# Gated DeltaNet stage: block sums and decay masks moved on VectorE, signs moved to ScalarE

## The chip, the cores and the metric

The kernel runs on one core of a Trainium2 chip. The metric is the device time of one execution in microseconds (us); the figure given is the median of several. All matrix products are in 32-bit floats.

## The reference

A backbone of two layers over 256 latent and 256 context tokens, D_MODEL 1024. Each layer is SwiGLU, token mixer, SwiGLU, with norms and modulation. The mixer of the first layer is a bidirectional gated DeltaNet with 8 heads of width 128. The change is in its scan, whose core for one head and one direction is, in the reference:

```python
Gamma = jnp.exp(jnp.where(incl, G[..., :, None] - G[..., None, :], -jnp.inf))
A = jnp.where(strict, jnp.einsum('nbhcd,nbhsd->nbhcs', kb, kc) * Gamma, 0.0)
Tinv = lax.linalg.triangular_solve(eye + A, jnp.broadcast_to(eye, A.shape), left_side=True,
                                   lower=True, unit_diagonal=True)
u = jnp.einsum('nbhcs,nbhse->nbhce', Tinv, vc * bc[..., None])
intra = jnp.einsum('nbhcd,nbhsd->nbhcs', qc, kc) * Gamma
```

and then a scan over chunks that carries a 128x128 state. The output is the latent stream.

## The kernel before

The kernel takes the 512 tokens in four chunks of 128 (the reference has chunks of 64; the result is the same) and both directions d = 0, 1 together. For each head it needs, in this order: the decays and their masked copies; the gram products of keys and queries (`gram_pair`, L1221); the unit-triangular inverse; the state scan over four chunks; the output.

**The inverse** is built in two steps. On VectorE, all 8x8 diagonal blocks are solved at once: GpSimd masks the blocks (`below`, L626), VectorE sums them into packed rows (`pack_rows`, L2661, one sum for each direction, and a subtraction, L2667), GpSimd spreads these (L640, L642), TensorE broadcasts them (`spread_blocks`, L1230), and VectorE runs `solve`: a copy (L2671) and seven pairs of small instructions (L2675, L2676), each behind the last. `place_base` writes the result as base blocks and transposes it (L2683, L2687). Then four levels double the block width: 8, 16, 32, 64. At each level q, TensorE forms a product (`level_p1`), VectorE masks or copies it (`mask_p1`), TensorE forms a second product (`level_y`), and the result, with its sign changed, enters the inverse (`update_y`). For widths 8 and 16 that is a subtraction and a transpose on packed blocks (L2714, L2715). At width 32 (q = 2) the packed blocks are unpacked into the full matrices `yy` and `tt_`: ScalarE places the diagonal blocks (`place_t`, `place_y`, L1818) and copies the transposed off-diagonal block with scale -1 (`copy_t`, L1837); VectorE writes the off-diagonal blocks with scale -1 (`negated`, L2707, 32 rows by 128, two for each direction). At width 64 (q = 3) VectorE writes the off-diagonal half (L2722, 64 rows by 256, one for each direction). "Signs" below are these instructions with scale -1.

**The rounds.** Every engine runs its own program of ten rounds (`rounds(delta_round)`). In round i four heads are in work: n = i prepares (decays, grams, block solve), g = i - 1 goes through the four levels, h = i - 2 goes through the state scan, f = i - 3 closes. Each round is a loop over q = 0 to 3, and in it the order of the work of the four heads on each engine is written out by hand. Heads are 0 to 7, so rounds 3 to 7 have all four, round 1 has n and g only, round 8 has no n, rounds 9 and 10 no n and no g. In round 1 (g = 0), TensorE also computes the last gate projections between the levels (`late_gate`, L1210), and ScalarE their exponentials (`gate_exp`).

What sets the order around the change are semaphores. `level_p1(g, q)` waits for the base blocks (q = 0), for VectorE's update of the level before, or, at q = 3, for `t_copied` and `y_updated`. `turn_v` and `turn_k` (TensorE transposes, L1305, L1296) wait for `intra_done`, since they write over the banks of the gram products that `make_intra` (L2602) reads. ScalarE's `scale_v` (L1848) and `copy_k` (L1843) follow, and TensorE's `spread_decays` of the next round (L1165) waits for them. ScalarE's `exp_sums` (L1700) and `bound` (L1706) follow that, and `gram_pair` waits for `bounded`. `new_values(h, 0)` (L1324), the start of a head's scan, waits for all the updates of its inverse. On GpSimd the order is: decays times beta (L621), the masked blocks (L626), the masked decays (L631), the two spreads (L640, L642), the decayed queries (L647). The solve's output goes to the same tile in which the level below width 32 works, so `place_base` waits for `place_y` of the head before.

Of the kernel before, what the change touches and what calls it, by code (L numbers as in the profile page):

```python
# [9 lines left out]
ALU = mybir.AluOpType  # L10
# [4 lines left out]
P = 128  # L15
# [198 lines left out]
def hybrid_backbone(nc, x, c, ctx_in, c_ctx, w_mod, b_mod, norm_pre, norm_post, ffn_w_in, ffn_w_out,  # L214
# [13 lines left out]
    with ExitStack() as ctx:  # L228
# [437 lines left out]
        def _(pe):  # L666
# [143 lines left out]
            for n, (kind, l, j) in enumerate(SUBS):  # L810
# [261 lines left out]
                if kind == "gdn":  # L1072
# [159 lines left out]
                    def level_p1(g, q):  # L1232
                        for d in range(2):
                            if q == 0:
                                of("base_done", g, 1, 1)
                            elif LEVELS[q] <= QUARTER:
                                of("y_updated", g, 2 * n_lev, 2 * (q - 1) + d + 1)
                            else:
                                of("t_copied", g, 2, d + 1)
                                of("y_updated", g, 2 * n_lev, 2 * (q - 1) + d + 1)  # L1240
# [328 lines left out]
        def _(act):  # L1569
# [70 lines left out]
            for n, (kind, l, j) in enumerate(SUBS):  # L1640
# [51 lines left out]
                if kind == "gdn":  # L1692
# [139 lines left out]

                    def copy_t(g):
                        for d in range(2):
                            r, o = quarters(d, d)
                            of("t_done", g, 2, d + 1)
                            fn(chunks(tt_[quarter_rows[o], d, :])[:, :, quarter_rows[r]],  # L1837
                               bank[quarter_rows[o], d, 3 * P:4 * P].rearrange("p (t c) -> p t c", t=NC), ACT.Copy, scale=-1.0
                               ).then_inc(S["t_copied"], 1)
# [36 lines left out]
                    def delta_round(n, g, h, f):  # L1876
# [3 lines left out]
                        for q in range(n_lev):  # L1880
# [11 lines left out]
                            if g is not None and q == 3:  # L1892
                                scale_v(g)
                                copy_k(g)
# [191 lines left out]
        def _(dve):  # L2086
# [223 lines left out]
            for n, (kind, l, j) in enumerate(SUBS):  # L2310
# [180 lines left out]
                if kind == "gdn":  # L2491
# [212 lines left out]
                    def negated(g, d, k):  # L2704

                        r, o = quarters(d, k)
                        return v_.tensor_scalar(chunks(yy[g % 2][quarter_rows[r], d, :])[:, :, quarter_rows[o]],  # L2707
                                                by_chunk(bank[quarter_rows[r], d, 2 * P:3 * P]), -1.0, None, ALU.mult)

                    def update_y(g, q):  # L2710
                        for d in range(2):
                            of("y_done", g, 2 * n_lev, 2 * q + d + 1)
                            if LEVELS[q] < QUARTER:
                                steps.link(v_.tensor_tensor(yq[d], yq[d], bank[:, d, 0:P], ALU.subtract))  # L2714
                                last = v_.transpose(tq[d], yq[d])  # L2715
                            elif LEVELS[q] == QUARTER:
                                last = negated(g, d, 1 - d)
                                last.then_inc(S["y_updated"], 1)
                                negated(g, d, d)
                                continue  # L2720
                            else:
                                last = v_.tensor_scalar(chunks(yy[g % 2][rows_of[d], d, :])[:, :, rows_of[1 - d]],  # L2722
                                                        by_chunk(bank[rows_of[d], d, 0:NC * HALF]), -1.0, None, ALU.mult)
                            last.then_inc(S["y_updated"], 1)
# [32 lines left out]
                    def delta_round(n, g, h, f):  # L2757
                        for q in range(n_lev):
# [4 lines left out]
                            if n is not None and q == 3:  # L2763
                                solve(n)
                            if n is not None and q == 1:
# [3 lines left out]
                            if g is not None:  # L2769
# [3 lines left out]
                            if n is not None and q == 2:  # L2773
                                pack_rows(n, 1)
                            if f is not None and q == 2:
                                close(f)
                            if n is not None and q == 2:
                                make_intra(n)
                            if g == 0 and q < 3:
                                gate_scale(4 + q)  # L2780
                        if n is not None:
                            place_base(n)
# [228 lines left out]
```

## Time and profile before

| | us |
|---|---|
| median of 3 runs | 2312.84 (2311.76 to 2315.14) |
| the profiled execution | 2312.73 |
| its span | 2311.0 |
| granted TensorE clock, mean of the span | 0.983 |
| TensorE matmul busy | 2217.4 (96%) |
| VectorE busy | 1343.4 (58%) |
| ScalarE busy | 609.2 (26%) |
| GpSimd busy | 169.7 (7%) |

The ten rounds of the delta stage run from about 695 to 917 us of the span. In the profile PE is TensorE's matmul, PEld its weight load, DVE VectorE, ACT ScalarE, POOL GpSimd; times of a row are microseconds from the span's start and durations in us, unless marked ns. A granted clock of 1.00 is 2.4 GHz, 0.50 is 1.2 GHz. In `128*128 128x256 f32` the first pair is the part of the array that is used. `[1.15 <-X]` says that the engine stood idle for 1.15 before this row, and that X released it.

### The profile page before, as it was taken

Reading aid. Unit: us, or ns where it says so; the run is one execution under the profiler, and the core shown is the slowest. Engines: PE = TensorE matmul, PEld = TensorE weight load, DVE = VectorE, ACT = ScalarE, POOL = GpSimd, SP = SyncE. Lnnn points to the kernel's source line nnn. Section 1 sums busy time; section 2 is a strip of 40 time slices with the busy share of each in tenths; the row PEclk is TensorE's granted clock in tenths of the full one; section 3 lists DMA queues with packets and bytes.
Section 4 is the critical chain, followed back from the end, with each engine's and each line's share of the span. In section 5 each row is a group of like instructions: output and inputs, shape, how many; then the busy total and the mean of one; then the engine's idle time right before and its main releaser. Section 6 shows DMA issues by size and latency. Waiting matters only on the chain.

```text
span 2311.0 us, 39267 instructions
## 1 busy us (share of the span) xinstructions
PE 2217.4 (96%) x15693; PEld 1916.7 (83%) x15693; DVE 1343.4 (58%) x2258; ACT 609.2 (26%) x1635; POOL 169.7 (7%) x236
## 2 busy tenths in 40 slices
PE   5999999999998888999999999999999999879998
PEld 3788889988865776888888998888899868569997
DVE  4377758666774885267775865767556421735521
ACT  2111111132344766321111123111111311632210
POOL 1100000000022441000000000000000000000000
PEclk7999999999999999999999999999999999989999
DMA  8555557532220000225554763455456332024462
GB/s 299 184 173 169 174 146 205 151 118 79 73 79 26 3 3 15 84 92 167 170 175 127 206 180 114 147 164 167 135 137 176 103 105 91 1 73 148 163 186 69
DMA packets 311486, 293.38 MB, mean 127 GB/s; under 512 B 6713, under 2 KB 292019, under 8 KB 311219
## 3 DMA queue, kind: packets, MB, share of 16 engines
q1 hardware_dynamic: 290611, 215.90, 31.4%
q0 software_dynamic: 20736, 75.51, 10.5%
q8 instruction: 102, 1.67, 0.3%
q14 instruction: 37, 0.30, 0.0%
HBM read 290.34 MB, written 1.05 MB: 126 GB/s over the span
## 4 chain that ended last, share of the span: by engine, by line
PE 89%; DVE 4%; ACT 3%; DMA 2%; issue 1%; SPq 0%; POOL 0%; DVEq 0%; POOLq 0%; ACTq 0%
PE bank L864 39%; PE bank L986 18%; PE bank L718 6%; PE bank L1092 5%; PE bank L1064 3%; PE bank L1445 2%; PE bank L828 2%; PE bank L1210 1%; PE bank L1147 1%; DMA mring<-in_w_mod 1%; PE bank L1221 1%; PE bank L696 1%; PE bank L1082 1%; ACT hs L1932 1%; PE bank L754 1%
## 5 line engine op out<-in xcount | busy, mean ns | idle before, releaser
L864 PE MATMUL bank<-hs,ring 128*128 128x256 f32 (+1 forms) x2112 | 446.1, 356 | 6.3 <-ACT hs L1617 5.1
L864 PEld LDWEIGHTS bank<-hs,ring 128*128 128x128 f32 x2112 | 365.5, 192 | 55.3 <-issue 11.3
L986 PE MATMUL bank<-big,ring 128*128 128x128 f32 x2904 | 330.2, 275 | 0.0
L986 PEld LDWEIGHTS bank<-big,ring 128*128 128x128 f32 x2904 | 327.4, 192 | 0.2
L864 PE MATMUL bank<-room,big 128*128 128x256 f32 (+1 forms) x1408 | 296.0, 353 | 0.0
L864 PEld LDWEIGHTS bank<-room,big 128*128 128x128 f32 x1408 | 242.4, 191 | 26.5
L2134 DVE SCALAR_TENSOR_TENSOR mring<-mring,cond 128x1024 f32<-128x1024 f32 x196 | 240.2, 1278 | 7.6 <-DMA mring<-in_w_mod 7.6
L603 POOL DMA_DIRECT2D mring<-in_w_mod x144 | 76.6, 532 | 1062.9 <-DVE mring L2128 488.3
L864 PE MATMUL bank<-room,ring 128*128 128x256 f32 (+1 forms) x704 | 149.3, 355 | 2.5 <-ACT room L1653 1.8
L864 PEld LDWEIGHTS bank<-room,ring 128*128 128x128 f32 x704 | 121.0, 190 | 20.0 <-ACT room L1653 6.8
L1657 ACT ACTIVATE room<-room 128x256 f32<-128x256 f32 (+1 forms) x88 | 34.3, 390 | 302.6 <-DVE room L2339 302.6
L2870 DVE TENSOR_TENSOR room<-room 128x256 f32<-128x256 f32 x70 | 29.5, 421 | 132.5 <-ACT room L1977 131.9
L2329 DVE TENSOR_TENSOR room<-room,bank 128x256 f32<-128x256 f32 (+1 forms) x88 | 34.0, 387 | 119.2 <-ACT room L1653 118.0
L986 PE MATMUL bank<-room,ring 128*128 128x128 f32 x792 | 95.1, 276 | 1.1 <-ACT cst L2042 1.1
L1653 ACT ACTIVATE room<-bank 128x256 f32<-128x256 f32 (+1 forms) x88 | 31.5, 358 | 237.5 <-PE bank L864 237.5
L986 PEld LDWEIGHTS bank<-room,ring 128*128 128x128 f32 x792 | 91.3, 192 | 1.7 <-ACT cst L2042 1.7
L718 PE MATMUL bank<-big,ring 128*128 128x256 f32 x384 | 89.4, 396 | 2.6 <-POOL big L662 1.8
L718 PEld LDWEIGHTS bank<-big,ring 128*128 128x128 f32 x384 | 76.1, 200 | 14.5 <-POOL big L662 2.2
L2334 DVE TENSOR_TENSOR big<-cst,bank 128x256 f32 (+3 forms) x88 | 33.9, 386 | 86.1 <-PE bank L864 86.0
L864 PE MATMUL bank<-hs,big 128*128 128x256 f32 (+1 forms) x384 | 80.8, 353 | 0.2 <-DVE room L2329 0.2
L2526 DVE SCALAR_TENSOR_TENSOR room<-room,prm 128x512 f32<-128x512 f32 x96 | 76.1, 792 | 3.1
L1064 PE MATMUL bank<-big,ring 128*128 128x256 f32 x352 | 77.3, 379 | 0.0
(355 smaller groups left out, 3252.2 us busy)
## 6 DMA issues: line engine op xcount, KB each, us to landing
ring<-in_ffn_w_in SPq DMA_DIRECT2D x88, 1024.0 KB, 5.7
ring<-in_ffn_w_out SPq DMA_DIRECT2D x56, 1408.0 KB, 7.2
mring<-in_w_mod POOLq DMA_DIRECT2D x144, 512.0 KB, 4.0
ring<-in_gdn_w_in SPq DMA_DIRECT2D x16, 1024.0 KB, 5.6
ring<-in_diff_w_in SPq DMA_DIRECT2D x12, 1024.0 KB, 5.2
ring<-in_gdn_w_out SPq DMA_DIRECT2D x4, 1024.0 KB, 5.5
ring<-in_diff_w_out SPq DMA_DIRECT2D x4, 1024.0 KB, 5.2
cst<-in_consts SPq DMA_DIRECT2D x1, 1344.0 KB, 10.2
```

Of the source, the lines that this page charges most:

```text
L603: pool.dma_start(mring[:, k % slots, :], w_mod[l, k * P:(k + 1) * P, ds(v * D + (i0 - 9 * l) * D, D)]).then_inc(m_landed[k % slots], 16)
L718: last = mm(bank[0:rows, r % 4, 0:cols], w[:, k, :], rhs(k), start=(k == 0), stop=(k == n_k - 1))
L828: last = mm(bank[:, g % 4, cols], w[:, k, :], hs[:, k, cols], start=(k == 0), stop=(k == KC - 1), skip_group_check=True)
L864: last = mm(bank[:, (g0 + b) % 4, 0:width], w[:, k, jj * P:(jj + 1) * P], rhs[:, k, 0:width], start=start and k == 0, stop=(k == KC // 2 - ...
L986: last = mm(bank[:, (go + b) % 4, 0:P], w[:, k, :], rhs[:, k, :], start=start and k == 0, stop=(k == FH - 1), skip_group_check=True)
L1064: last = mm(bank[:, g % 4, 0:LAT], w[:, k, :], big[:, k, cols], start=(k == 0), stop=(k == FC - 1))
L1092: last = mm(bank[:, (g0 + b) % 4, 0:LAT], w[:, k, :], rhs[:, k, :], start=start and k == 0, stop=(k == KC // 2 - 1), skip_group_check=True)
L1445: last = mm(bank[:, g % 4, 0:256], hs[:, k, t * P:(t + 1) * P], slot(ux, KC, 256)[:, k, :], start=(k == 0), stop=(k == KC - 1))
L1657: fn(u2c[c % 2][:, 0:width], u2c[c % 2][:, 0:width], ACT.Silu).then_inc(S["gate2_done"], 1)
L2134: last = v_.scalar_tensor_tensor(m_acc[:, v, :], w, scalar, m_acc[:, v, :], ALU.mult, ALU.add)
L2329: v_.tensor_tensor(u4c[c % 2][:, 0:width], u4c[c % 2][:, 0:width], bank[:, (g0 + 3) % 4, 0:width], ALU.add).then_inc(S["c22_added"], 1)
L2526: last = v_.scalar_tensor_tensor(o, conv_in[:, u % 4, :, t:t + LAT], tap(t), o, ALU.mult, ALU.add)
```

## The change

On VectorE, both block sums now stand right behind the copies of level 2; the state update comes ahead of the width-32 signs; the decay masks (`make_intra`) move from the end of q = 2 to q = 3, ahead of the solve; the base blocks move from the end of the round to right behind the solve. Of the width-32 signs VectorE keeps one for each direction, the other goes into ScalarE's `copy_t`, ahead of the signal `t_copied`. The last level's signs go to a new function `place_last` on ScalarE, ahead of `scale_v`. On TensorE the waits follow: level 3's first product waits for `t_copied` alone, and the first level waits also for the last signs of the head before. What is computed stays the same.

```diff
--- before.py
+++ after.py
@@ -1233,11 +1233,12 @@
                         for d in range(2):
                             if q == 0:
                                 of("base_done", g, 1, 1)
+                                if g:
+                                    of("y_updated", g - 1, 2 * n_lev, 2 * (n_lev - 1) + d + 1)
                             elif LEVELS[q] <= QUARTER:
                                 of("y_updated", g, 2 * n_lev, 2 * (q - 1) + d + 1)
                             else:
                                 of("t_copied", g, 2, d + 1)
-                                of("y_updated", g, 2 * n_lev, 2 * (q - 1) + d + 1)
                             for t in range(NC):
                                 if LEVELS[q] < QUARTER:
                                     for r in range(4):
@@ -1830,12 +1831,23 @@
                                 last = in_place(yy[g % 2], yq[d], d, r)
                             last.then_inc(S["y_placed"], 1)
 
+                    def place_last(g):
+                        for d in range(2):
+                            of("y_done", g, 2 * n_lev, 2 * (n_lev - 1) + d + 1)
+                            fn(chunks(yy[g % 2][rows_of[d], d, :])[:, :, rows_of[1 - d]],
+                               bank[rows_of[d], d, 0:NC * HALF].rearrange("p (t c) -> p t c", t=NC), ACT.Copy, scale=-1.0
+                               ).then_inc(S["y_updated"], 1)
+
                     def copy_t(g):
                         for d in range(2):
                             r, o = quarters(d, d)
                             of("t_done", g, 2, d + 1)
                             fn(chunks(tt_[quarter_rows[o], d, :])[:, :, quarter_rows[r]],
-                               bank[quarter_rows[o], d, 3 * P:4 * P].rearrange("p (t c) -> p t c", t=NC), ACT.Copy, scale=-1.0
+                               bank[quarter_rows[o], d, 3 * P:4 * P].rearrange("p (t c) -> p t c", t=NC), ACT.Copy, scale=-1.0)
+                            r, o = quarters(d, 1 - d)
+                            of("y_done", g, 2 * n_lev, 2 * (n_lev - 2) + d + 1)
+                            fn(chunks(yy[g % 2][quarter_rows[r], d, :])[:, :, quarter_rows[o]],
+                               bank[quarter_rows[r], d, 2 * P:3 * P].rearrange("p (t c) -> p t c", t=NC), ACT.Copy, scale=-1.0
                                ).then_inc(S["t_copied"], 1)
 
                     def copy_k(g):
@@ -1890,6 +1902,7 @@
                                 copy_t(g)
                                 place_y(g)
                             if g is not None and q == 3:
+                                place_last(g)
                                 scale_v(g)
                                 copy_k(g)
                             if n is not None and q == 0:
@@ -2701,12 +2714,6 @@
                                 last = v_.tensor_copy(p1m[rows_of[1 - d], d, 0:NC * HALF], bank[rows_of[1 - d], d, 0:NC * HALF])
                             last.then_inc(S["p1_masked"], 1)
 
-                    def negated(g, d, k):
-
-                        r, o = quarters(d, k)
-                        return v_.tensor_scalar(chunks(yy[g % 2][quarter_rows[r], d, :])[:, :, quarter_rows[o]],
-                                                by_chunk(bank[quarter_rows[r], d, 2 * P:3 * P]), -1.0, None, ALU.mult)
-
                     def update_y(g, q):
                         for d in range(2):
                             of("y_done", g, 2 * n_lev, 2 * q + d + 1)
@@ -2714,13 +2721,9 @@
                                 steps.link(v_.tensor_tensor(yq[d], yq[d], bank[:, d, 0:P], ALU.subtract))
                                 last = v_.transpose(tq[d], yq[d])
                             elif LEVELS[q] == QUARTER:
-                                last = negated(g, d, 1 - d)
-                                last.then_inc(S["y_updated"], 1)
-                                negated(g, d, d)
-                                continue
-                            else:
-                                last = v_.tensor_scalar(chunks(yy[g % 2][rows_of[d], d, :])[:, :, rows_of[1 - d]],
-                                                        by_chunk(bank[rows_of[d], d, 0:NC * HALF]), -1.0, None, ALU.mult)
+                                r, o = quarters(d, d)
+                                last = v_.tensor_scalar(chunks(yy[g % 2][quarter_rows[r], d, :])[:, :, quarter_rows[o]],
+                                                        by_chunk(bank[quarter_rows[r], d, 2 * P:3 * P]), -1.0, None, ALU.mult)
                             last.then_inc(S["y_updated"], 1)
 
                     def rest(h, st):
@@ -2761,25 +2764,24 @@
                             if g is not None:
                                 mask_p1(g, q)
                             if n is not None and q == 3:
+                                make_intra(n)
                                 solve(n)
+                                place_base(n)
                             if n is not None and q == 1:
                                 make_m2(n)
                             if n is not None and q == 2:
                                 pack_rows(n, 0)
-                            if g is not None:
+                                pack_rows(n, 1)
+                            if g is not None and q < 2:
                                 update_y(g, q)
                             if h is not None and q < NC - 1:
                                 next_state(h, q)
-                            if n is not None and q == 2:
-                                pack_rows(n, 1)
+                            if g is not None and q == 2:
+                                update_y(g, q)
                             if f is not None and q == 2:
                                 close(f)
-                            if n is not None and q == 2:
-                                make_intra(n)
                             if g == 0 and q < 3:
                                 gate_scale(4 + q)
-                        if n is not None:
-                            place_base(n)
                         if n == 1:
 
                             dve.wait_ge(S["acc_done"], gz + KC)
```

## Rows read from the trace of the kernel before

**Rows 1.** Page, the chain that ended last, shares of the span by engine.
```profile
PE 89%; DVE 4%; ACT 3%; DMA 2%; issue 1%; SPq 0%; POOL 0%; DVEq 0%; POOLq 0%; ACTq 0%
```

**Rows 2.** Windows: length; busy (count) of PE, PEld, DVE, ACT, POOL; clock; DMA share, GB/s.
```profile
722.40:731.00 8.60, 8.60 (x27) 4.22 (x28) 0.95 (x3) 2.68 (x9) 0.00 (x0) 0.61 0.00 0
812.20:836.40 24.20, 21.25 (x470) 18.14 (x473) 19.78 (x59) 17.11 (x64) 10.69 (x10) 1.00 0.01 3
```

**Rows 3.** Chain that ended last, in order of time: start, us, what.
```profile
764.26 0.46 DVE room L2687
...
883.29 0.46 DVE room L2687
```

**Rows 4.** Timeline of VectorE, round 5: start, us, line, operation, count, idle before.
```profile
824.00 1.22 DVE L2707 TENSOR_SCALAR room<-bank 32x128 f32<-32x128 f32 x4
...
826.08 1.06 DVE L2661 TENSOR_REDUCE room<-ring 128x32 f32<-128x512 f32 x1
...
827.92 1.28 DVE L2602 TENSOR_TENSOR hs<-bank,hs 128x512 f32<-128x512 f32 x2
...
830.55 0.65 DVE L2671 COPY room<-cst 128x64 f32<-128x64 f32 x1
...
834.49 0.88 DVE L2722 TENSOR_SCALAR room<-bank 64x256 f32<-64x256 f32 x2
835.40 0.43 DVE L2683 TENSOR_TENSOR room<-room,cst 128x256 f32<-128x256 f32 x1
```

**Rows 5.** Timeline of GpSimd, round 5.
```profile
827.49 0.63 POOL L640 TENSOR_TENSOR ring<-room,cst 128x256 f32<-128x256 f32 x1 [3.51 <-DVE room L2667]
...
828.66 2.50 POOL L647 TENSOR_TENSOR hs<-big,hs 128x512 f32<-128x512 f32 x2
```

**Rows 6.** Timeline of VectorE, rounds 1 and 2: the copy that opens the solve.
```profile
724.37 0.18 DVE L2671 COPY room<-cst 128x64 f32<-128x64 f32 x1
...
758.36 1.24 DVE L2671 COPY room<-cst 128x64 f32<-128x64 f32 x1
```

**Rows 7.** Timeline of TensorE, round 5 and the start of round 6.
```profile
826.64 0.96 PE L1254 MATMUL bank<-room,mring 64*64 64x64 f32 x16
828.75 1.12 PE L1230 MATMUL bank<-ring,cst 128*128 128x512 f32 x2 [1.15 <-POOL ring L642]
...
833.18 1.14 PE L1165 MATMUL bank<-cst,pack 128*128 128x128 f32 x8
...
836.36 0.75 PE L1244 MATMUL bank<-room,mring 32*32 32x32 f32 x64 [0.16 <-DVE room L2687]
...
837.92 1.99 PE L1221 MATMUL bank<-big 128*128 128x256 f32 x8
```

**Rows 8.** Lines L1837 and L1843: count, ns min/median/max, first and last start, form.
```profile
L1837 ACT ACTIVATE room<-bank x16: 268/268/269, 722.1 to 895.3; 32x128 f32<-32x128 f32 x16
...
L1843 ACT ACTIVATE room<-bank x4: 614/614/615, 738.5 to 880.4; 128x512 f32<-128x512 f32 x4
```

**Rows 9.** Timeline of ScalarE, round 5.
```profile
825.33 0.56 ACT L1837 ACTIVATE room<-bank 32x128 f32<-32x128 f32 x2
...
831.98 1.14 ACT L1848 ACTIVATE big<-bank,pack 128x128 f32<-128x128 f32 x4 [1.22 <-PE bank L1305]
...
834.85 2.17 ACT L1706 ACTIVATE mring<-bank,pack 128x128 f32<-128x128 f32 x8
```

**Rows 10.** Timeline of TensorE, round 1.
```profile
722.39 1.60 PE L1254 MATMUL bank<-room,mring 64*64 64x64 f32 x16 [3.54 <-ACT room L1837]
723.92 6.23 PE L1210 MATMUL bank<-hs,ring 128*128 128x512 f32 x8
...
731.82 3.70 PE L1210 MATMUL bank<-hs,ring 128*128 128x512 f32 x8
...
738.66 1.52 PE L1165 MATMUL bank<-cst,pack 128*128 128x128 f32 x8 [2.26 <-ACT big L1848]
```

**Rows 11.** Timeline of ScalarE, round 8.
```profile
895.62 2.55 ACT L1818 ACTIVATE hs<-room 32x128 f32<-32x128 f32 x8
```

## The prediction

> **What bounds it now.** I read the page first. TensorE holds 89% of the chain that ended last, VectorE 4% [rows 1]; that is an average over stages, and says nothing of the stage that the diff touches. The windows by stage come next: in one round of the delta stage (812.2 to 836.4) all of TensorE, VectorE and ScalarE work 17 to 21 of 24.2 us, and the granted clock is 1.00 [rows 2]. No engine is full, so the chain decides. In it a round ends each time with VectorE's solve, the last level's two signs (L2722), the base blocks (L2683) and their transpose (L2687), and the next round's first level (L1244) starts behind them. From the transpose of round 2 to that of round 7, 764.26 to 883.29, are five rounds: 23.8 us each [rows 3]. So in rounds 2 to 7 what VectorE does from level 2 on, without a pause, sets the length; in the first third of a round it waits for TensorE, and nothing of that third changes. Rounds 1 (gate projections on TensorE between the levels) and 8 (no solve) are of another kind.
>
> **The steady round (rounds 3 to 7), in round 5's times.** I lay VectorE's work in the new order from the copies of level 2 on (end at 822.9).
> 1. Both block sums now stand there, 1.06 and a step each [rows 4], with their subtraction, until 825.3: about the time that the first block sum and four signs took before (825.2). The state update behind them came at 825.23 and comes at 825.3; its second half waits for TensorE until 825.82 as before. Their input, GpSimd's masked blocks, was ready before the first sum ran, so nothing new is waited for.
> 2. The four width-32 signs take 1.22 [rows 4], 0.305 each. Two remain, two go to ScalarE: **0.61** saved.
> 3. The last level's two signs go to ScalarE: from their start at 834.49 to that of the base blocks at 835.40, **0.91** saved [rows 4].
> 4. The solve's first instruction, a copy of 64 columns, takes 0.65 in round 5 (start 830.55, next 831.23), 1.24 in round 2, but 0.18 in round 1 [rows 4, 6]. In round 5 it ends just where GpSimd's product for the decayed queries ends (828.66 + 2.50 = 831.16), in round 1 GpSimd had long done its own [rows 4, 5, 6]. That product stands behind two short spreads (from 827.49 on) that wait for the block sums [rows 5]. The second sum ended at 827.14 and now ends at 825.06, so the spreads and the product move up by 2.08, to an end near 829.1. The copy will start at about 829.95 and find GpSimd idle: 0.68 falls to 0.20, **0.48** saved. Bounds: 0 and 0.48.
> 5. The decay masks (1.20 for two, L2602) move from ahead of the third state step to ahead of the solve. VectorE pays the same there, so 0. Who waits for them? TensorE's transposes of v and k. By this count the masks end at 829.95, and TensorE gets there at 830.2: the block broadcast (L1230), which stood 1.15 waiting for GpSimd until 828.75 [rows 7], starts at once at 827.6, and new values and level 3 follow without a gap. Their cover is thin, 0.2.
> 6. The base blocks stand right behind the solve; they need the level-3 placement on ScalarE done (near 829.0) and start near 833.4. Cost 0. The first level's new wait for the last signs on ScalarE (done near 830.7) is long over by then.
>
> Steps 2 to 4 sum to 2.00: the next round's first level starts at 834.37, not 836.36 [rows 7].
>
> **What ScalarE takes on.** Width-32 signs: 32x128 from PSUM has rows, 0.268, and a pair takes 0.56 [rows 8, 9]. The 64x256 sign has none; between 0.268 (128 columns) and 0.614 (512 columns) [rows 8] the line by columns gives 0.383, which I take, as duration follows columns; the ends stay for the range. Queued behind the width-32 signs: the placements of the diagonal (eight, 2.55), now ending at 829.03, ahead of level 3's second half at 829.6. Ahead of level 3's first product, the copies end at 826.45, and TensorE arrives at 826.64 [rows 7]: hidden by 0.19. Queued behind the last signs: the scaling of v, the copy of k, and the next round's exponentials. The signs end near 830.65, v is turned at 830.87, so they are hidden by 0.2. The scaling ends at 832.0 where it ended at 833.1 [rows 9], so the spreading of decays (833.18) comes at 832.07: 1.1 earlier, while the round's start comes 2.0 earlier. **ScalarE thus lags 0.9 more behind the start of the round.** Its bound step (L1706, 834.85 for 2.17) ended 0.66 behind the start and will end 1.55 behind it; the gram products that wait for it started 1.56 behind it (837.92 less 836.36) [rows 7, 9]. That is zero cover; I book 0.1. The decays that it makes after that feed GpSimd and through it VectorE's products, whose slack is larger than this lag: 0. A steady round gains **1.9**, five of them **9.5**.
>
> **Round 2.** 0.61 + 0.91, and from the copy 1.07 (1.27 less 0.20) = 2.59. Level 3's product on TensorE is then waited for briefly, about 0.2 by its rows there: **2.4** saved. GpSimd's product would end at about 757.85 and the copy start at about 757.8: no more than 0.1.
>
> **Round 1 loses.** The chain goes through ScalarE twice. Level 3 waited for the copies until 722.39 [rows 10]; each direction's signal now comes behind one more sign: **+0.28**. At its end ScalarE's last gate exponential, the scaling of v, and the spreading at 738.66 follow one another [rows 10]; the two last-level signs stand between, 2 x 0.383: **+0.77**. VectorE's 0.91 is no gain there, since its base blocks were early, and the moved masks fall into 6 us of its idle time.
>
> **Round 8 loses a little.** There is no solve, so the last signs are on the path either way. The placements on ScalarE ended at 898.17 [rows 11], and level 3's second half started near then; two signs ahead of them move it by 0.5, and v's scaling with it: **+0.5**. No DMA and no queue of SP is touched; GpSimd only starts earlier; what follows the stage moves as a whole.
>
> **Sum.** -9.5 - 2.4 + 0.28 + 0.77 + 0.5 = -10.35. The profiled execution took 2312.73 (its span 2311.0 and 1.73 around it): 2302.4. It lies 0.1 below the median of the runs, so 2302.4 stands against 2312.84.
>
> The Trainium skill says (GPSIMD Engine Reference, Specifications) that GpSimd shares its SBUF interfaces with VectorE, and contends with VectorE instructions that have two SBUF inputs as well as with those in a two-port mode. By that rule too the copy is freed. It could speak against the change, since GpSimd's product now runs beside other VectorE work; but each VectorE instruction of that stretch has an operand in PSUM, so the rule adds nothing to the sum, and the trace agrees so far as the copy alone of the instructions beside that product differs from one round to the next; no row here has an instruction with two SBUF inputs beside it.
>
> **Rivals.**
> *A. The copy stays slow* (its wait comes from something else, or GpSimd moves up less). For it: only the ends agree, no row shows the cause. Against: the 0.18 of round 1. Time: 5 x 0.48 + 1.07 = 3.5 less gain, 2305.9.
> *B. ScalarE becomes the bound at the round's head.* For it: the cover ahead of the gram products is zero. If a 64x256 sign costs 0.614, the pair is 0.46 longer; 0.2 is covered, 0.26 is paid in six rounds and 0.46 in round 1: 2304.4. With as much again of lag from late transposes: 2306.5.
> *C. Nothing left to gain*: another wait of the first third grows by what the end of the round saves (say a chain over ScalarE from one round's v to the next round's gram products is 1.5 longer than I count). For it: three engines all work 17 to 21 us of a round. Against: each wait counted above. Time: 2311 to 2314.
> *D. Slower: TensorE's clock.* In round 1 the pause of 3.54 ahead of level 3 was followed by 8.6 us at a mean clock of 0.61, between 1.2 and 2.4 GHz and so for most of them at 1.2 [rows 2, 10]. There the gate products took 6.23 for eight, against 3.70 a little later, and level 3 took 1.60, against 0.96 in round 5 [rows 7, 10]: a fall costs 3.2. The change lengthens this pause by 0.28 and the one of 2.26 at 736.4 by 0.77. If the new pattern of pauses made the clock fall once a round, six falls would cost 19 and the time would be 2321. It decides from four falls on (10.35 / 3.2). Against it: in steady rounds the longest pause was 1.2 at a clock of 1.00 [rows 2, 7], and it gets shorter.
> The Trainium skill has a rule that speaks for D (TensorE: Matmul & The Clock Gate, HAM oscillation): a matmul stream with recurring waits can swing between the two clock levels. The trace agrees in round 1 and not in rounds 3 to 7; by the rule alone D would be as likely as not, and the rows make it unlikely.
>
> **Chances.** Forecast 0.72, A 0.09, B 0.10, C 0.05, D 0.04. A run-to-run difference of about 0.2% (4.6 us) is what a measurement of this kernel can tell. Faster by more: forecast, A, B: 0.91. Within 0.2%: 0.05. Slower: 0.04. The range starts below the forecast by one fall of the clock that may fail to come in round 1 (3.2) and the 0.1 per round, 2299, and goes up to B's second figure and a little over A, 2307.
>
> **What would show it.** Rounds 3 to 7 at 21.9 each between the transposes L2687; the solve's copy at 0.18 in rounds 3 to 7; the 64x256 signs on ScalarE near 0.38; no wait of TensorE for GpSimd ahead of the block broadcast; gram products 1.6 behind the start of the round; VectorE busy some 14 us less in the whole (two signs of 0.29 and two of 0.42 in eight rounds, and the copies' 3.5). I am wrong if the gram products start over 2 behind it, if the transposes of v wait for the masks for over 0.3, or if the clock is below 1.00 in a steady round.

## The result and the profile after

The changed kernel takes 2299.04 us (median of four executions, 2296.22 to 2301.93) against 2312.3 (median of four of the kernel before). The ratio of the two is put at 0.9938, with a 95% interval of 0.9923 to 0.9953: 14.3 us faster, 10.9 to 17.8 (the medians are 13.3 apart). The forecast was 10.35 us faster and a time of 2302.4, in a range that began at 2299.0. The sign was right and the gain was larger than forecast; the profiled execution itself took 2301.93, within half a microsecond of the forecast. The 3 us and more between the forecast and the medians are what the experiments had to find.

The page after (span and instructions; busy time of the engines; the chain that ended last by engine):

```profile
span 2300.2 us, 39265 instructions
...
PE 2217.7 (96%) x15693; PEld 1917.3 (83%) x15693; DVE 1328.2 (58%) x2226; ACT 618.6 (27%) x1667; POOL 169.7 (7%) x236
...
PE 90%; ACT 3%; DVE 3%; DMA 2%; issue 1%; SPq 0%; POOL 0%; DVEq 0%; POOLq 0%; ACTq 0%
```

VectorE is busy 15.2 less (forecast 14), ScalarE 9.4 more. Line numbers have moved: L2725 is the width-32 sign that VectorE kept, L1849 the one that ScalarE took, L1837 the last level's signs, L2684 the copy that opens the solve, L2700 the transpose of the base blocks, L1245 the first level.

VectorE's timeline in round 5 (from the transpose at 806.83 to that at 828.55), beside [rows 4]:

```profile
817.57 2.07 DVE L2674 TENSOR_REDUCE room<-ring 128x32 f32<-128x512 f32 x2
...
820.50 0.35 DVE L2743 SCALAR_TENSOR_TENSOR hs<-hs,pack,bank 128x128 f32<-128x128 f32 x1 [0.32 <-PE bank L1341]
820.76 0.60 DVE L2725 TENSOR_SCALAR room<-bank 32x128 f32<-32x128 f32 x2
...
823.43 1.27 DVE L2615 TENSOR_TENSOR hs<-bank,hs 128x512 f32<-128x512 f32 x2
824.63 0.18 DVE L2684 COPY room<-cst 128x64 f32<-128x64 f32 x1
...
828.10 0.43 DVE L2696 TENSOR_TENSOR room<-room,cst 128x256 f32<-128x256 f32 x1
828.55 0.45 DVE L2700 STREAM_TRANSPOSE room<-room 128x256 f32<-128x256 f32 x1
```

Each term of the forecast's steady round is there: two signs in place of four, the copy at 0.18, no last-level signs. The round takes 21.72, where an undisturbed round of before took 23.72: 2.00 less, which is the sum of steps 2 to 4. Rounds 3 and 4 of this profile are longer, 22.19 and 21.97. ScalarE and TensorE in the same round:

```profile
820.45 0.27 ACT L1849 ACTIVATE room<-bank 32x128 f32<-32x128 f32 x1
...
824.42 0.78 ACT L1837 ACTIVATE room<-bank 64x256 f32<-64x256 f32 x2
825.45 1.14 ACT L1860 ACTIVATE big<-bank,pack 128x128 f32<-128x128 f32 x4 [0.25 <-PE bank L1306]
```

```profile
822.23 1.11 PE L1230 MATMUL bank<-ring,cst 128*128 128x512 f32 x2
...
829.05 0.75 PE L1245 MATMUL bank<-room,mring 32*32 32x32 f32 x64 [0.82 <-DVE room L2700]
...
830.61 1.56 PE L1221 MATMUL bank<-big 128*128 128x256 f32 x6
```

The pair of 64x256 signs (L1837) takes 0.78 (twice 0.383 was 0.77), the scaling of v still waits for TensorE behind it, the block broadcast waits for nobody, and the gram products start 1.56 behind the round's start, as in [rows 7].

Round 1, TensorE's timeline, beside [rows 10]:

```profile
722.15 1.60 PE L1255 MATMUL bank<-room,mring 64*64 64x64 f32 x16 [3.81 <-ACT room L1849]
723.68 6.26 PE L1210 MATMUL bank<-hs,ring 128*128 128x512 f32 x8
...
739.27 1.97 PE L1165 MATMUL bank<-cst,pack 128*128 128x128 f32 x8 [3.07 <-ACT big L1860]
```

The two pauses grew from 3.54 to 3.81 and from 2.26 to 3.07: +0.27 and +0.81, where +0.28 and +0.77 were forecast.

### The profile page after: what moved, and what is told of

The parts are those of the page before. It is cut to its first block, busy times and chain, and to the rows that moved or that the text cites. A ratio compares the mean times of both kernels' runs of the same rounds, so it can differ in the third digit from the quotient of the medians.

```text
span 2300.2 us, 39265 instructions
## 1 busy us (share of the span) xinstructions
PE 2217.7 (96%) x15693; PEld 1917.3 (83%) x15693; DVE 1328.2 (58%) x2226; ACT 618.6 (27%) x1667; POOL 169.7 (7%) x236
## 4 chain that ended last, share of the span: by engine, by line
PE 90%; ACT 3%; DVE 3%; DMA 2%; issue 1%; SPq 0%; POOL 0%; DVEq 0%; POOLq 0%; ACTq 0%
PE bank L864 40%; PE bank L986 18%; PE bank L718 6%; PE bank L1092 5%; PE bank L1064 3%; PE bank L1446 2%; PE bank L828 2%; PE bank L1210 1%; PE bank L1147 1%; DMA mring<-in_w_mod 1%; PE bank L1221 1%; PE bank L696 1%; PE bank L1082 1%; ACT hs L1945 1%; PE bank L754 1%
```

## The experiments

### More profiles of both kernels, to see what differs from one execution to the next

The changed kernel once more, with five executions:

> The changed kernel once more. Its profiled execution took 2301.9, near the 2302.4 forecast, while the median of its four executions is 2299.0 and their granted clocks went from 0.982 to 0.986. Theory (the clock): the missing 3 us are no work of the delta rounds but half-clock stretches of TensorE that come in some executions and not in others. Then the times again spread over 5 us, go down as the mean clock goes up, and a profile with a time of 2296 to 2299 shows rounds 3 to 7 at 21.7 as in the first profile, and a stretch at half clock less elsewhere. Rival (the rounds): in the faster executions the rounds themselves are shorter; then a faster profile shows rounds under 21.5 at the same clock outside them.

2298.78 median (2296.16 to 2300.25), ratio 0.9937 (0.9923 to 0.9950). The profiled execution took 2299.89. The rival falls: rounds 3 to 7 are not shorter than in the first profile but 1.3 longer (110.62 against 109.35). Nor are they at 21.7 throughout, as the theory had it: rounds 3 to 5 take 22.2, 22.8 and 22.2. What is shorter is rounds 1 and 2, 68.0 against 70.3, with round 2 at a clock of 1.00 where it was 0.94. Then single profiles of the kernel before:

> The kernel before, unchanged, for a second profile. Theory (the clock in the rounds): the first profile of before (clock 1.00 in rounds 2 to 7, 23.7 a round) was a favourable one; in most executions of before one or two of these rounds run partly at 1.2 GHz, and the change, which shortens TensorE's pauses, loses fewer. Then this profile may show a window 742 to 875 at a mean clock of 0.96 to 0.98 and one or more rounds of 24.2 or more. Rival (the clock falls elsewhere or equally): rounds 2 to 7 are at 1.00 again, and what varies is round 1 and the stretches outside.

> The same kernel again, the same two expectations: a third profile of before, to be read for the clock of 742 to 875 and the length of each round.

> The kernel before for a fourth profile. Theory: more likely than not one of rounds 3 to 7 runs partly at 1.2 GHz (mean clock of the five rounds 0.97 to 0.99) and is longer than 24.1. Rival: all at 1.00, 118.6 to 119.1 in the sum.

and two more of the changed kernel:

> The changed kernel for a third profile. Over all executions so far, 0.001 of mean granted clock goes with 1.24 us, and the changed kernel runs at a mean clock of 0.9844 against 0.9817. Theory (the change also keeps TensorE's clock up in the rounds): rounds 3 to 7 run at a clock of 1.00 and take 109 to 111 us, as in the two profiles before, while three of five profiles with the old pauses show 0.97 there. Rival (chance): rounds 3 to 7 show a fall as often as before, a window at 0.97 to 0.99 and a round over 23.

> The changed kernel for a fourth profile, with the same two expectations.

The single times were 2308.53, 2315.83 and 2313.28 for before, 2301.71 and 2300.43 for the changed kernel. Windows of rounds of before, first of its third profile (765.35 is round 3, 812.81 round 5), then of its fourth (round 6); columns as in [rows 2]:

```profile
765.35:789.07 23.72, 21.03 (x469) 18.03 (x468) 19.59 (x59) 16.78 (x63) 10.70 (x10) 1.00 0.01 3
812.81:838.00 25.19, 23.72 (x469) 19.98 (x468) 19.56 (x59) 15.55 (x59) 10.68 (x10) 0.86 0.01 3
```

```profile
833.78:859.14 25.36, 22.66 (x469) 19.20 (x468) 19.58 (x59) 16.95 (x64) 10.69 (x10) 0.93 0.01 3
```

A round takes 23.72 at a clock of 1.00, and 1.5 to 1.7 more when a part of it runs at the lower level. The profile that the forecast read had no such round. Rounds 3 to 7 as one window, the fourth profile of before, and the first and second of the changed kernel:

```profile
762.01:882.90 120.89, 105.94 (x2324) 90.55 (x2324) 98.33 (x296) 82.68 (x304) 53.49 (x50) 0.99 0.01 3
```

```profile
762.67:872.02 109.35, 102.69 (x2324) 88.52 (x2323) 88.23 (x275) 91.16 (x333) 53.51 (x50) 1.00 0.01 3
```

```profile
761.15:871.77 110.62, 103.09 (x2324) 88.72 (x2323) 88.59 (x276) 91.16 (x333) 53.49 (x50) 1.00 0.01 3
```

By part of the stage, means over four profiles of each kernel (the single values in brackets):

| part | before | changed | difference | forecast |
|---|---|---|---|---|
| rounds 1 and 2 | 71.5 (71.4, 71.2, 70.3, 73.0) | 69.7 (70.3, 68.0, 70.3, 70.4) | -1.8 | -1.35 |
| rounds 3 to 7 | 120.3 (119.0, 120.4, 120.7, 120.9) | 110.2 (109.4, 110.6, 110.2, 110.6) | -10.1 | -9.5 |
| from round 8 to the output projection | 36.7 | 37.1 | +0.4 | +0.5 |

Three of four profiles of before lose clock in rounds 3 to 7 (1.00, 0.99, 0.97, 0.99); the four of the changed kernel show 1.00. Their profiled executions are 11.6 apart (means 2312.6 and 2301.0), and all of that lies in the stage: what stands ahead of it and behind it sums to 2082.5 before and 2082.3 after. The kernel's other seven executions are faster still, 2298.15 in the mean; no profile shows those. What the result does give for every execution is the mean granted clock. Over 52 executions of before it is 0.9817 in the mean (mean time 2312.5), over 11 of the changed kernel 0.9843 (2299.2). Within kernels, over all those run here, 0.001 of clock goes with 1.21 us (1.02 to 1.40). So 0.0026 goes with 3.2 us of the 13.3 between the means, and 10.1 are left, against the forecast's 10.35. That is a regression, and no proof that the clock is the cause.

Not every round of the changed kernel is at 21.7 either. Two things make rounds 3 to 5 longer. In round 3 TensorE waits 0.36 to 0.38 for ScalarE's bound step, in all four profiles. In rounds 4 and 5 it stands still in the middle of a level's products, for 0.2 to 0.6 in round 4 (three profiles of four) and 0.3 in round 5 (the same three), with nothing in the profile that it waits for ("issue"). The kernel before has such a stop too, in the round that the forecast read, round 5: 0.32, for a round of 24.16. In the changed kernel's second profile, then before:

```profile
785.88 0.38 PE L1278 MATMUL bank<-room 32*32 32x32 f32 x21 [0.58 <-issue]
```

```profile
819.58 0.25 PE L1277 MATMUL bank<-room 32*32 32x32 f32 x4 [0.32 <-issue]
```

What these stops are, and why there are more of them in the changed kernel's profiles, no run here shows.

### The pauses of before, filled

```diff
-                        of("rows_spread", n, 2, 2)
                         if n > 2:
                             of("head_closed", n - 3, 1, 2)
+                            for t in range(4):
+                                mm(bank[:, 5 - n % 2, ch[t]], ident, ident, start=True, stop=True)
+                        of("rows_spread", n, 2, 2)
...
+                                elif h < 7:
+                                    for t in range(4):
+                                        mm(bank[:, 2, P:2 * P], ident, ident, start=True, stop=True)
```

> The kernel before, with TensorE kept at work in its two pauses of each steady round: four 128x128 products (0.9 us) whose result is overwritten ahead of the block broadcast, and four ahead of a head's first new values. No work on the path is added or taken away where the pauses are 1.15 and 1.19. Theory (pauses let the clock fall in the rounds of before): the mean clock rises from 0.982 to 0.984 or more and the time falls by 1 to 4 us. Rival (the clock of the rounds has nothing to do with it): same time within 1 us, or up to 2 us more where the filling is in the way.

This kernel's output is wrong: the extra products, or the wait that moved behind them, spoil a value that is still needed, and no run shows which. It is no kernel to use, and it is read here for its times and clock alone.

2311.83 against 2313.1, ratio 0.9997 (0.9988 to 1.0006). The mean clock of its 11 executions is 0.9835, against 0.9818 for the 15 of before beside them. Its profile, rounds 3 to 7 as one window:

```profile
766.18:884.88 118.70, 112.43 (x2405) 97.81 (x2404) 97.99 (x295) 82.39 (x304) 53.55 (x50) 1.00 0.01 3
```

All five rounds lie at 23.72 to 23.75, the undisturbed length. So with TensorE at work in most of the pauses (0.46 is left of the 1.15) the mean clock is higher, as the theory said, though short of the 0.984 it asked for. The gain in time did not show: the interval runs from 2.8 faster to 1.4 slower. The clock's share of the result is therefore supported by the clocks, and not shown in time by any run.

### The copy that opens the solve

The kernel before, with GpSimd's product ahead of its two spreads:

```diff
+                for d in range(2):
+                    of("expg_done", n, 2, d + 1)
+                    nc.gpsimd.tensor_tensor(qdec[n % 3][:, d, :], ...).then_inc(S["qdec_done"], 1)
                 of("rows_ready", n, 1, 1)
...
-                for d in range(2):
-                    of("expg_done", n, 2, d + 1)
...
```

> The kernel before, with one edit on GpSimd: the product for the decayed queries stands ahead of the two spreads, so that it runs before VectorE's copy. VectorE's program is unchanged. Theory (the copy waits for GpSimd's product): the copy takes 0.18 in rounds 2 to 7, and the kernel is 3.5 us faster (5 x 0.48 + 1.07), about 2308.8 against 2312.3. Rival A (the copy's length has another cause, such as what stands ahead of it on VectorE): the copy stays at 0.65 and 1.24 and the time stays at 2312.3.

2307.97 against 2312.3, ratio 0.9982 (0.9973 to 0.9991): 4.2 us faster, 2.1 to 6.2, for 3.5 expected. GpSimd and VectorE in one round (GpSimd's product is L637 here):

```profile
798.33 2.54 POOL L637 TENSOR_TENSOR room<-big,room 128x512 f32<-128x512 f32 x2
```

```profile
804.53 0.18 DVE L2671 COPY room<-cst 128x64 f32<-128x64 f32 x1
```

The copy takes 0.18 in all rounds, with VectorE's program unchanged. Rival A falls: the copy waited for GpSimd's product. (The copy ahead of round 1 falls too, from 0.67 to 0.19, which the 3.5 had left out; in the changed kernel it stays at 0.66.) In this profile rounds 3 and 6 show a clock of 0.93.

### Order alone, signs alone

The kernel before with the new order on VectorE, all signs left there:

```diff
                             if n is not None and q == 3:
+                                make_intra(n)
                                 solve(n)
...
                                 pack_rows(n, 0)
-                            if g is not None:
+                                pack_rows(n, 1)
+                            if g is not None and q < 2:
                                 update_y(g, q)
...
+                            if g is not None and q >= 2:
+                                update_y(g, q)
```

> The kernel before with only the new order on VectorE: both block sums ahead, state update ahead of the width-32 signs, decay masks ahead of the solve; all signs stay on VectorE and the base blocks stay behind the last signs. By the forecast's terms only the copy's 0.48 (1.07 in round 2) is gained: 3.5 us, about 2308.8, and the rest of the order is worth 0. Rival: the order is worth more than its copy, by waits that it frees (over 5 us faster), or the later signs delay level 3's first product and eat it (no gain).

2310.19, ratio 0.9991 (0.9982 to 1.0): 2.1 us faster, at most 4.2. Copies are at 0.18, undisturbed rounds at 23.37, or 0.35 less than 23.72 rather than 0.48. The profiled execution (2305.67) was the fastest of the eleven.

The changed kernel with VectorE's old order:

```diff
-                                make_intra(n)
                                 solve(n)
-                                place_base(n)
...
-                                pack_rows(n, 1)
-                            if g is not None and q < 2:
+                            if g is not None and q < 3:
                                 update_y(g, q)
...
```

> The changed kernel with VectorE's order of before, so that only the signs have moved to ScalarE. Forecast's terms: 0.61 + 0.91 in six rounds is 9.1 gained, less 1.05 lost in round 1 and 0.5 in round 8: 7.6 us faster than before, about 2304.7; the copy stays slow (near 0.6 in rounds 3 to 7), since block sums, GpSimd's product and copy all move up together. Rival (the moved signs cost on ScalarE what they save on VectorE, as the scaling of v is behind them): under 4 us.

2307.2, ratio 0.9978 (0.9968 to 0.9988): 5.1 us faster, 2.8 to 7.4, short of 7.6. Its profiled execution was the slowest of nine, 2315.02, with rounds 5 and 6 at a clock of 0.93. Rounds 3 and 4, at 1.00, take 22.8 and 23.1, not the 22.2 that 23.72 less 0.61 and 0.91 would give. VectorE in round 4:

```profile
801.28 1.07 DVE L2674 TENSOR_REDUCE room<-ring 128x32 f32<-128x512 f32 x1
802.27 0.60 DVE L2725 TENSOR_SCALAR hs<-bank 32x128 f32<-32x128 f32 x2
803.54 0.35 DVE L2743 SCALAR_TENSOR_TENSOR hs<-hs,pack,bank 128x128 f32<-128x128 f32 x1 [0.67 <-PE bank L1341]
...
808.94 0.67 DVE L2684 COPY room<-cst 128x64 f32<-128x64 f32 x1
```

Two signs are gone, and VectorE stands 0.67 for the state update's product in their place: the 0.61 is not saved at all. The copy stays slow. So the two parts, 2.1 and 5.1 us, make 7.2 of 14. The next run puts the second block sum where the signs were and leaves the rest, and is 11.1 faster than before: what was missing is that place.

### Signs and block sums, masks and base blocks at their old places

```diff
-                                make_intra(n)
                                 solve(n)
-                                place_base(n)
...
+                            if n is not None and q == 2:
+                                make_intra(n)
...
+                        if n is not None:
+                            place_base(n)
```

> The changed kernel with the decay masks and the base blocks back at their old places on VectorE, so that what is changed against before is the signs and the place of the block sums. With the signs alone a steady round took 22.8 to 23.1, since VectorE then stood 0.67 waiting for the state update's product, where the signs had been. Theory (the second block sum fills that wait, and masks and base blocks are worth 0): 21.7 to 21.9 a round, and a time within 2 us of the changed kernel, 2298.8. Rival (masks behind or base blocks ahead are what counts): 22.5 or more a round, 2303 or more.

2301.56, ratio 0.9952 (0.9939 to 0.9966), 2.8 us behind the changed kernel's 2298.78, and rounds at 22.25: between the two expectations, in round and in time. The intervals of the two kernels overlap, so the difference rests on the rounds. VectorE's wait at the head of a round, in this kernel and then in the changed one:

```profile
834.60 0.29 DVE L2740 COPY hs<-bank 128x128 f32<-128x128 f32 x1 [1.77 <-PE bank L1341]
```

```profile
811.14 0.29 DVE L2740 COPY hs<-bank 128x128 f32<-128x128 f32 x1 [1.25 <-PE bank L1341]
```

VectorE has the same work in both. With the masks ahead of the third state step, new values and level 3 on TensorE come later (level 3's second product at 847.78, some 18.0 behind the transpose; in the changed kernel at 823.71, 16.9 behind it). ScalarE's signs, scaling and exponentials follow them, and the gram products at the next round's head wait 0.45 for ScalarE's bound step, where they wait for nothing in the changed kernel's later rounds. The base blocks play no part: with the signs gone, nothing stands between the solve and the end of VectorE's loop, so their two places are the same. The masks' new place is worth 0.5 a round, by way of ScalarE. In the changed kernel the same wait is left in round 3 alone, here in its third profile:

```profile
764.95 1.99 PE L1221 MATMUL bank<-big 128*128 128x256 f32 x8 [0.36 <-ACT mring L1707]
```

### A version that is faster than both

The changed kernel, with round 1's last gate projection moved into TensorE's pause:

```diff
+                            if g == 0 and q == 3:
+                                late_gate(4 + q, 0)
                             if g is not None:
                                 level_p1(g, q)
-                            if g == 0 and q:
+                            if g == 0 and 0 < q < 3:
                                 late_gate(4 + q, 0)
...
+                            if g == 0 and q == 3:
+                                late_gate(4 + q, 1)
                             if g is not None:
                                 level_y(g, q)
-                            if g == 0 and q:
+                            if g == 0 and 0 < q < 3:
                                 late_gate(4 + q, 1)
```

> The changed kernel, with the last gate projection of round 1 moved: its first half ahead of level 3's first product, into TensorE's pause of 3.5, and its second half ahead of level 3's second product. By the forecast's terms for round 1: the pause of 3.5 is filled with work that stood behind it (3.5 gained), the fall of the clock behind it does not come (3.2 gained), and ScalarE's gate exponential leaves the path: in all 5 to 9 us faster than the changed kernel, about 2292. Rival (the gate's exponential on ScalarE delays the level copies, or the clock falls elsewhere instead): under 3.5.

2294.31, ratio 0.9920 (0.9906 to 0.9933): 18.5 us faster than before, and 4.5 below the changed kernel's 2298.78, between the two expectations (5 to 9, and under 3.5 for the rival). The intervals of the two ratios overlap, so the difference rests on the profile. TensorE in round 1:

```profile
714.79 7.13 PE L1210 MATMUL bank<-hs,ring 128*128 128x512 f32 x16
722.30 1.11 PE L1255 MATMUL bank<-room,mring 64*64 64x64 f32 x16 [0.38 <-ACT room L1853]
723.35 1.13 PE L1230 MATMUL bank<-ring,cst 128*128 128x512 f32 x2
724.31 3.60 PE L1210 MATMUL bank<-hs,ring 128*128 128x512 f32 x8
```

Round 1 as one window, here and in the changed kernel:

```profile
692.52:728.94 36.42, 34.67 (x444) 18.33 (x443) 18.76 (x50) 15.43 (x39) 10.64 (x10) 1.00 0.14 45
```

```profile
692.37:734.62 42.25, 37.07 (x441) 19.41 (x440) 18.75 (x49) 14.47 (x37) 10.62 (x10) 0.92 0.12 39
```

The pause of 3.81 is 0.38, the clock of the round is 1.00, and eight gate products take 3.60 where 6.26 stood. This is the clearest case of a pause and a fall that go together, though in one profile of this kernel: the one is filled, and in that round the other does not come. From the first transpose to the output projection this profile is 7.4 shorter than the changed kernel's, of which the medians keep 4.5.

## Why the prediction was right, and where it was not

- **What bounds a steady round: right.** The chain over VectorE's second half, with steps 2 to 4 at 0.61 + 0.91 + 0.48 = 2.00; undisturbed rounds went from 23.72 to 21.72.
- **Step 1 and step 2 belong together,** which the forecast laid out but did not say: without the second block sum in their place the signs' 0.61 goes into a wait of 0.67. The terms hold for the whole change and not for its parts.
- **Step 4: shown** by the kernel with GpSimd's product ahead. The copy fell from 0.65 to 0.18. The Trainium skill's rule (GPSIMD Engine Reference, Specifications), that GpSimd contends over its shared SBUF interfaces with VectorE instructions in a two-port mode or with two SBUF inputs, agrees with that if the copy, which has one input, runs in a two-port mode; no run here shows its mode.
- **Step 5 was wrong in its size.** Masks "VectorE pays the same there, so 0": they are worth 0.5 a round, since their old place holds up TensorE and with it ScalarE. This does not come on top of the 2.00: with the masks at their old place a round takes 22.25, and only 1.47 of the 2.00 is there.
- **ScalarE's lag was sized about right, and its place was not.** "That is zero cover; I book 0.1", or 0.5 in five rounds. The wait is there in round 3 alone and makes it 0.45 longer; rival B's mechanism goes no further. Rounds 3 to 7 took 110.2 in the mean of four profiles, 1.5 more than five of 21.73. The rest of the 1.5 lies in rounds 4 and 5, mostly in the stops of TensorE for which the profile names nothing. The forecast had one such stop in its mean round of 23.8 and no term for more.
- **Rounds 1 and 8: right**: +0.27 and +0.81 for +0.28 and +0.77, and +0.4 for +0.5.
- **The lower end of the range was added up wrong.** One fall that fails to come (3.2) and 0.1 in each of five rounds take 2302.4 to 2298.7, not to 2299.
- **The step that failed is the last line of the sum.** "It lies 0.1 below the median of the runs, so 2302.4 stands against 2312.84" took the profiled execution for a typical one of both kernels. Its time was typical, its clock in rounds 3 to 7 was not: it showed 1.00 there, where the three later profiles of before have a stretch at the lower level and are 1.4 to 1.9 us longer. The forecast thus put at nothing, without a reason, the falls that the change takes away. What the runs showed in its place: 1.3 us in rounds 3 to 7 (120.3 in the mean of four profiles for the 119.0 that it read), and, over all executions, 3.2 us of the difference that go with the mean clock. Against the changed kernel's own profile the forecast was 0.5 off, against the median 3.4. The falls in rounds 3 to 7 are seen in profiles; the rest lies in executions without one, and why their clock is higher stays open.
- **Rival D had the mechanism and the wrong sign.** It asked whether new pauses make the clock fall, and noted that the steady rounds' pauses get shorter, but only as a reason against a loss. The same sentence was a reason for a gain. The Trainium skill's rule (TensorE: Matmul & The Clock Gate, HAM oscillation), that a matmul stream with recurring waits can swing between the levels, was dismissed for rounds 3 to 7 on one profile; the three later profiles of before agree with it, at 0.99, 0.97 and 0.99.

What stays open is how much of the 14 us is the clock. About 3 us go with it by the regression; the run made to raise the clock alone, whose output is wrong, showed no gain outside its interval.

## What to carry to other kernels

Where several engines hand work on in a ring, moving work off the bounding engine gains only if something else can fill the slot up to its next wait: lay the whole new order out, do not add up parts. Before a sum is set against a median, look at whether the profiled execution had the clock of the others; a change that shortens TensorE's pauses may have a term for falls that no longer come, which one profile of before need not show (here up to 3 us of 2300, not proven). Filling a long pause of TensorE with work that stands just behind it can pay more than the pause: here 3.4 us of it were filled and round 1 became 5.8 shorter.

## What the runs showed of the hardware that I had not expected

With no TensorE pause in rounds 3 to 6 of before longer than 1.23, the clock still fell in some of them and in some executions: a round took 23.72 at 1.00 and 25.19 at a mean of 0.86. Six of the fourteen profiles have the pause of 1.15 ahead of the block broadcast (four of before, GpSimd's product ahead, the signs alone), and five of these show one or two of rounds 3 to 7 at 0.86 to 0.93. The other eight (four of the changed kernel, and those with filled pauses, new order, signs and sums, and gate ahead) have 0.46 or less there, and all show 1.00, the new order alone among them, which keeps a pause of 1.33 ahead of a head's new values. That is a count, not a rule: the mean clock of all executions follows it loosely (0.9817 before, 0.9825 for the order alone, 0.9836 for the signs alone, 0.9843 for the changed kernel).

VectorE's 64-column copy in SBUF took 0.65 or 1.24 beside GpSimd's product and 0.18 without it, while the decay masks, products with an operand in PSUM, took 0.68 each whether that product ran beside them or not.
